# Two edits in a one-core layer kernel: where the experts' down bias is added, and how the first loads and modulation weights are laid out

## The chip, the cores and the metric

The kernel runs on one core of one Trainium2 chip. The metric is the device time of one execution in microseconds (us). All data are 32-bit floats in HBM at the start, and the output goes back to HBM.

## The reference, cut to what matters

The program computes two transformer layers on 256 tokens of width 1024. The first layer normalises x, modulates it with vectors that come from a conditioning row c, mixes tokens (an RWKV recurrence and a block attention), and ends in a mixture of 32 experts with 4 experts for each token. The second layer has another attention and a feed-forward of width 4096. What the change touches is this:

```python
mods = jax.nn.silu(c) @ w_ada + b_ada                  # (1, 6*1024)
shift1, scale1, gate1, shift2, scale2, gate2 = jnp.split(mods[:, None, :], 6, axis=-1)
h = rms_norm(x, norm1_g) * (1.0 + scale1) + shift1
proj = h @ w_in
...
def expert_block(args):                                # rows of one expert
    tok, e = args
    gu = h[tok] @ w_gate_up[e] + b_gate_up[e]
    gate = jnp.minimum(gu[:, :D_FF], SWIGLU_LIMIT)
    up = jnp.clip(gu[:, D_FF:], -SWIGLU_LIMIT, SWIGLU_LIMIT)
    act = (up + 1.0) * gate * jax.nn.sigmoid(SWIGLU_ALPHA * gate)
    return act @ w_down[e] + b_down[e]
...
# each row times its routing weight, summed over a token's four experts
```

## The kernel before, in words

Every engine has its own hand-written program, and the engines meet at semaphores. The order of the work is the order of each program; no planner stands behind it. SyncE (SP) issues nearly all weight loads on its own DMA queue, and ScalarE (ACT) issues the small ones on a second queue. Both queues are served by the same 16 DMA engines.

**The front.** ACT issues x first (L1419), then 21 small loads of parameter rows into `prow` and `prow2` (L1422 to L1438), then the four pieces of the LoRA weights `wl` (L1440), the router weights `w_rout` (L1444, rows of 128 bytes), its bias, and the experts' first biases `bgu` (L1447). Only then does it compute. SP walks through the list `PRO` of 22 pieces (L308, L362): first the four pieces of w_ada that hold shift1 and scale1, then w_in, with the other pieces of w_ada between. They go through four slots of a ring in SBUF, so piece n waits until piece n-4 is used (`pro_freed`, L355, on `halves_used`), and mem_2 is loaded ahead of piece 4 (L368). Each of the first four pieces is a block of 512 columns of all 1024 rows of w_ada: 128 partitions by 8 row segments of 2 KB, some 2 MB.

TensorE (PE) turns x (L572), waits for all parameter rows and turns them (L577), adds up the squares of x (L584), and then multiplies silu(c) by each piece of w_ada as it arrives (L592 to L610). The silu is 32 equal columns, so that four matmuls for four row blocks k run side by side in four column groups of the array; their four partial sums are turned and added by VectorE (DVE) with a reduce for each piece (`ada_sum`, L1797). When the modulation is whole (`mods_ready`), ACT and DVE scale the normalised x (L1467, L1811), and the first projection (`proj`, L627, matmuls at L643) starts when the first piece of w_in is there.

**The expert loop.** After the router, the kernel works through 32 items, one for each expert (64 rows of capacity; every expert needs one pass here). The ring has nine slots of 2 MB and an expert has six pieces, four of w_gate_up and two of w_down. The first nine pieces are loaded ahead (L395 ff.), the others when a slot is freed (`freed`, on `e_gu` and `e_down`). For one item PE runs the bias of gate and up (L1103: a row `one_e` with a single one picks row e of `bgu`), gate and up (L1110), the gather of the item after next (L1047), the scatter of the item before (`scatter`, L1058: it multiplies the 64 rows by their routing weights and adds them into banks 4 to 7 of PSUM), some transposes, and the down projection (L1146). DVE makes the row `one_e` for the next item with `expert_row` (L2087), ahead of its wait for `e_selturn` in the loop (L2156).

**The down bias** is added once, before the loop: the routing weights of all 32 experts are turned (L1075 to L1078), DVE copies them to `gt` (L2127), and eight matmuls with 32 rows (`down_bias`, L1068 and L1084, matmul at L1070) start the sums of banks 4 to 7 with b_down times the routing weights. Just before and after stand the first gather, `turn_x(1)`, and the waits for `npass_ready` and `wtT_ready`:

```python
            gather(1)
            pe.wait_ge(*at("wt_ready"))
            for i in range(TT):
                last = tr(B(1)[0:E_N, i * P:(i + 1) * P], wt[:, i, :])
            last.then_inc(*mark("wt_turned"))
            turn_x(1)
            pe.wait_ge(*at("npass_ready"))
            pe.wait_ge(S("ada_summed"), 7)
            pe.wait_ge(*at("wtT_ready"))
            pe.wait_ge(S("b_down_in"), 16)
            down_bias(range(KT))
```

A matmul in 32-bit floats is two records in the profile. Transposes of all stages have the line of their helper, L568, and loads that of theirs, L353 for SP and L1412 for ACT.

## Time and profile before

| | us |
|---|---|
| median of 3 runs (1594.67 to 1599.12) | 1597.52 |
| the profiled execution, its own time | 1595.94 |
| its span in the profile | 1594.2 |
| PE busy | 1512.1 (95%) |
| DVE busy | 369.2 (23%) |
| ACT busy | 285.0 (18%) |
| DMA | 503.24 MB, mean 316 GB/s |

The page names the busy time of each engine, and PE leads with 95%. Yet its share is an average over stages, and the matmuls' ends are modelled. The kernel has three large stages: up to about 320 us the first layer up to the router, then the expert loop to 1236 us, and then the second layer. Times in the rows below are microseconds from the start of the span; "<-" names what ended an idle time. A row by stretches has start and end, the length, the busy time and number of instructions of PE, its weight loads, DVE, ACT and POOL in this order (or of PE alone), then the granted clock of TensorE as a share of 2.4 GHz, the busy share of the DMA engines, and the GB/s they moved. The record of the granted clock begins at 23.7 us; the rows show 1.00 before that whatever the engine did.

### The profile page before, as it was taken

To read this page: it belongs to the slowest core of one execution; us is meant where nothing else is said; L and a number is where in the kernel's file an instruction comes from. 1 tells how busy PE (TensorE), PEld (TensorE's weight loads), DVE (VectorE), ACT (ScalarE), POOL (GpSimd) and SP (SyncE) were. 2 spreads that over 40 slices of the span, in tenths; PEclk is the share of its full clock that TensorE was granted. 3 is DMA by queue.
4 is the path that set the end of the run, shared out by engine and by line. 5 is a ranking of instruction groups with operands and counts; after the bars stand their busy time and mean duration, and the time that the engine had idled before them with its cause. 6 is when DMAs were issued, how large, how long until landed. Compare 5 with 4: busy or idle time off the path is not lost.

```text
span 1594.2 us, 20391 instructions
## 1 busy us (share of the span) xinstructions
PE 1512.1 (95%) x8382; PEld 780.1 (49%) x8383; DVE 369.2 (23%) x712; ACT 285.0 (18%) x451; POOL 34.6 (2%) x86
## 2 busy tenths in 40 slices
PE   5999899999999999999999989989999999999998
PEld 3876686733333333333333333333333875888443
DVE  2476442322111111111112112112111233301003
ACT  2123411311111111111111111111111231100000
POOL 5000120000000000000000000000000000000000
PEclk9999998999999999999999999999999999999999
DMA  9856203889999999999999999999999641444420
GB/s 347 293 208 224 94 4 116 372 339 429 428 428 429 428 428 428 430 428 429 428 428 428 429 430 428 429 428 428 428 430 411 244 153 59 160 157 159 158 105 27
DMA packets 75038, 503.24 MB, mean 316 GB/s; under 512 B 5278, under 2 KB 8496, under 8 KB 50416
## 3 DMA queue, kind: packets, MB, share of 16 engines
q1 hardware_dynamic: 72240, 498.22, 76.1%
q10 hardware_dynamic: 2752, 4.34, 0.8%
q8 instruction: 37, 0.61, 0.2%
q14 instruction: 9, 0.07, 0.0%
HBM read 501.49 MB, written 1.05 MB: 315 GB/s over the span
## 4 chain that ended last, share of the span: by engine, by line
PE 70%; DMA 25%; DVE 2%; ACT 1%; ACTq 1%; issue 0%; SPq 0%; DVEq 0%
DMA ring<-in_w_gate_up 24%; PE psum L1110 15%; PE psum L1146 10%; PE psum L1375 6%; PE psum L1390 5%; PE psum L643 5%; PE psum L1197 3%; PE psum L1063 3%; PE psum L568 2%; PE psum L1047 2%; PE psum L981 2%; PE psum L1332 2%; PE psum L1400 2%; PE psum L1103 1%; PE psum L690 1%; PE psum L1347 1%
## 5 line engine op out<-in xcount | busy, mean ns | idle before, releaser
L1110 PE MATMUL psum<-ring,work 128*64 128x512 f32 x2048 | 456.5, 597 | 40.3 <-DMA ring<-in_w_gate_up 40.3
L1110 PEld LDWEIGHTS psum<-ring,work 128*64 128x64 f32 x2048 | 140.8, 137 | 354.7 <-issue 272.7
L1146 PE MATMUL psum<-ring,work 128*64 128x512 f32 x1024 | 226.8, 595 | 1.0
L2145 DVE TENSOR_SCALAR work<-psum 128x512 f32<-128x512 f32 x32 | 22.1, 692 | 623.7 <-PE psum L1110 623.7
L1146 PEld LDWEIGHTS psum<-ring,work 128*64 128x64 f32 x1024 | 70.8, 137 | 136.4 <-issue 127.8
L1657 ACT ACTIVATE work<-work 128x512 f32<-128x512 f32 x32 | 20.1, 629 | 440.7 <-DVE work L2145 440.7
L1375 PE MATMUL psum<-xT,ring 128*128 128x256 f32 x448 | 96.9, 379 | 0.0
L1375 PEld LDWEIGHTS psum<-xT,ring 128*128 128x128 f32 x448 | 85.0, 190 | 11.5
L1390 PE MATMUL psum<-ring 128*128 128x512 f32 x192 | 82.6, 592 | 0.0
L643 PE MATMUL psum<-ring 128*128 128x256 f32 (+1 forms) x368 | 81.0, 382 | 1.1 <-DMA ring<-in_w_in 1.1
L643 PEld LDWEIGHTS psum<-ring 128*128 128x128 f32 (+1 forms) x368 | 68.9, 188 | 14.0 <-issue 2.1
L1063 PE MATMUL psum<-work 64*128 64x256 f32 x528 | 65.9, 389 | 0.7 <-ACT work L1663 0.7
L1063 PEld LDWEIGHTS psum<-work 64*128 64x128 f32 x528 | 48.3, 186 | 31.9 <-issue 26.0
L1047 PE MATMUL psum<-tok,work 128*64 128x512 f32 x264 | 62.3, 592 | 0.3 <-DVE work L2083 0.3
L1390 PEld LDWEIGHTS psum<-ring 128*128 128x128 f32 x192 | 36.5, 190 | 45.5 <-issue 45.4
L1663 ACT ACTIVATE work<-psum 128x512 f32<-128x512 f32 x32 | 19.1, 598 | 209.1 <-PE psum L1146 209.1
L1197 PE MATMUL psum<-xT,ring 128*128 128x256 f32 x224 | 49.7, 381 | 0.7 <-DVE xT L2164 0.7
L1643 ACT ACTIVATE yT<-psum 128x512 f32<-128x512 f32 x33 | 35.1, 1064 | 70.1 <-PE psum L1047 70.1
L1197 PEld LDWEIGHTS psum<-xT,ring 128*128 128x128 f32 x224 | 42.1, 190 | 7.6 <-issue 1.8
L1657 ACT ACT_TABLE_LOAD x32 | 41.1, 1283 | 0.9 <-issue 0.3
L1047 PEld LDWEIGHTS psum<-tok,work 128*64 128x64 f32 x264 | 18.9, 137 | 37.5 <-issue 37.5
L1103 PE MATMUL psum<-bgu,work 32*64 32x512 f32 x256 | 35.7, 627 | 0.0
(434 smaller groups left out, 1265.1 us busy)
## 6 DMA issues: line engine op xcount, KB each, us to landing
ring<-in_w_gate_up SPq DMA_DIRECT2D x128, 2048.0 KB, 36.5
ring<-in_w_down SPq DMA_DIRECT2D x72, 2048.0 KB, 39.7
ring<-in_w_ada SPq DMA_DIRECT2D x12, 2048.0 KB, 12.6
ring<-in_w_up SPq DMA_DIRECT2D x8, 2048.0 KB, 7.5
ring<-in_w_in SPq DMA_DIRECT2D x6, 2048.0 KB, 8.3
ring<-in_w_out SPq DMA_DIRECT2D x4, 2048.0 KB, 8.4
ring<-in_w_in_sb SPq DMA_DIRECT2D x4, 2048.0 KB, 22.8
ring<-in_w_mem_kv SPq DMA_DIRECT2D x1, 2048.0 KB, 9.2
```

The source lines that it names most:

```text
L568: return nc.tensor.transpose(o, i, ident[0:n, 0:n])
L643: last = mm(bank2(bank)[0:m, jj, :], w[:, k, j * P:j * P + m], hT[:, k, :], start=k == 0, stop=k == KT - 1)
L1047: last = mm(B(0)[CAP * h:CAP * (h + 1), :], sel[:, ti, :], tok[:, ti, 512 * h:512 * (h + 1)], start=ti == 0, stop=ti == TT - 1)
L1063: last = mm(bank2(4 + m // 2)[:, m % 2, :], ye[CAP * h:CAP * (h + 1), c * P:(c + 1) * P], selT[CAP * h:CAP * (h + 1), :], start=False, sto ...
L1103: mm(B(1 + u)[CAP * h:CAP * (h + 1), :], one_e[r0:r0 + E_N, :], bgu[r0:r0 + E_N, :], start=True, stop=False)
L1110: ins = mm(B(1 + u)[CAP * h:CAP * (h + 1), :], xe[:, k % 4, k // 4, :], w[:, k % 2, c0:c0 + 512], start=False, stop=k == KT - 1)
L1146: last = mm(B(3)[CAP * h:CAP * (h + 1), :], act[:, k % 4, k // 4, :], w[:, k % 4, 512 * h:512 * (h + 1)], start=k == 0, stop=k == KT - 1)
L1197: last = mm(bank2(b)[:, jj, :], post_w(n)[:, k, c0 + jj * P:c0 + (jj + 1) * P], xT[:, k, :], start=k == 0, stop=k == KT - 1)
L1375: last = mm(bank2(b)[:, jj, :], w[:, k, c0:c0 + P], xT[:, k, :], start=k == 0, stop=k == KT - 1)
L1390: last = mm(B(4 + 2 * i + h), hid[:, k, i * P:(i + 1) * P], down_piece(n)[:, kk_, 512 * h:512 * (h + 1)], start=k == 0, stop=False)
L1643: A(by_four(x_tm), B(0).rearrange("p (q c) -> p q c", c=4), ACT.Copy).then_inc(S("e_xtm"), 1)
L1657: A(sgm, gt, ACT.Sigmoid, scale=1.702).then_inc(S("e_sig"), 1)
```

## The change

It has two parts.

In the expert loop the eight matmuls ahead of the loop, the transposes of the routing weights and DVE's copy of them go. Instead each item starts the sums of its down projection with two matmuls, one for each half of the columns: the row `one_e` picks row e of `b_down`. `one_e` is therefore needed until the down projection has begun, and DVE writes the next one at the end of its round, after a wait on `e_down`. Banks 4 to 7 now start with a product of zeros (`zero`, with the cleared `selT` and `ye`): two such matmuls before `turn_x(1)` and two after it, with the wait for `npass_ready` moved ahead of `turn_x(1)`.

In the front x moves from ACT's queue to the head of SP's, and ACT's queue begins with c, b_ada and norm1_g. These 64 rows are turned first, ahead of x, and ACT makes the sigmoid of c ahead of its copies of x. The other parameter rows follow into a tile of their own and are turned after the modulation. The LoRA weights go to SP's queue behind piece 5, and the router weights, its bias and `bgu` behind piece 9. Each of the first four pieces of w_ada is now 256 whole rows cut at 2048 columns, row segments of 8 KB. The four column groups of one bank now hold four different blocks of 512 columns and add up over all k, so one copy, four transposes and one addition on DVE take the place of four rounds of them.

The diff, without the lists of milestone names, the counters that follow from them, and the loads that only change their tile:

```diff
+N_FIRST = ROW["norm2_g"]
...
-        def pe_ada(x):
-            return x if x < 4 else x - 5
+        def ada_rows(s):
+            return ring[:, s, :].rearrange("p (k n) -> p k n", k=2)
...
+            load(tok[:, :, :], a["x"][0].rearrange("(i p) d -> p i d", p=P), S("x_in"))
...
-                if kind == "ada":
+                if kind == "ada" and i < 4:
+                    load(ada_rows(s), a["w_ada"][0, 2 * P * i:2 * P * (i + 1), 0:2048].rearrange("(k p) n -> p k n", p=P),
+                         S(f"pro_in{s}"))
+                elif kind == "ada":
                     load(slot8(s), chunk_cols(a["w_ada"][0], 512 * i, 512), S(f"pro_in{s}"))
...
+                if n == 5:
+                    load(wl[0:LOW, 0, :], a["rwkv_w_up"][0], S("wl_in"))
+                    load(wl[LOW:P, 0, :], a["rwkv_a_up"][0], S("wl_in"))
+                    load(wl[:, 1, :], a["rwkv_g_up"][0, 0:P, :], S("wl_in"))
+                    load(wl[0:GLOW - P, 2, :], a["rwkv_g_up"][0, P:GLOW, :], S("wl_in"))
+                if n == 9:
+                    load(w_rout[:, :, :], a["w_router"][0].rearrange("(k p) n -> p k n", p=P), S("rout_in"))
+                    load(b_rout[:, :], a["b_router"], S("rout_in"))
+                    for q in range(4):
+                        load(bgu[E_N * q:E_N * (q + 1), :], a["b_gate_up"][0, :, 512 * q:512 * (q + 1)], S("bgu_in"))
...
-            g_.memset(prow, 0.0).then_inc(S("pool_stage"), 1)
+            g_.memset(prow3, 0.0).then_inc(S("pool_stage"), 1)
...
+            pe.wait_ge(S("par_first_in"), 16 * 3)
+            tr(B(1)[:, 0:N_FIRST], prow[0:N_FIRST, :], N_FIRST).then_inc(*mark("par_turned"))
             pe.wait_ge(S("x_in"), 16)
             for b in range(4):
                 for k in (2 * b, 2 * b + 1):
                     for i in range(TT):
                         last = tr(bank2(4 + b)[:, k % 2, i * P:(i + 1) * P], tok[:, i, k * P:(k + 1) * P])
                 last.then_inc(S("x_turned"), 1)
-            pe.wait_ge(S("par_in"), 16 * N_PAR_DMA)
-            tr(B(1)[:, 0:N_ROWS], prow[0:N_ROWS, :], N_ROWS)
-            last = tr(B(1)[:, N_ROWS:N_ROWS + N_ROWS2], prow2[0:N_ROWS2, :], N_ROWS2)
-            last.then_inc(*mark("par_turned"))
...
-            for n in range(5):
-                if n < 4:
-                    arrived(n)
-                    if n >= 2:
-                        pe.wait_ge(S("ada_copied"), n - 1)
-                    w = slot8(pro_slot(n))
-                    for k in range(KT):
-                        q = 32 * (k % 4)
-                        last = mm(B([0, 4][n % 2])[q:q + 32, :], silc[:, k, :], w[:, k, :], start=k < 4, stop=k >= 4)
-                        if k % 4 == 3:
-                            last.then_inc(S("halves_used"), 1)
-                if n >= 1:
-                    m = n - 1
-                    pe.wait_ge(S("ada_copied"), m + 1)
-                    if m >= 2:
-                        pe.wait_ge(S("ada_summed"), m - 1)
-                    for j in range(4):
-                        last = tr(B(5 + m % 2)[:, j * P:(j + 1) * P], ada_sb[m % 2][:, j * P:(j + 1) * P])
-                    last.then_inc(S("ada_turned"), 1)
+            for n in range(4):
+                arrived(n)
+                w = ada_rows(pro_slot(n))
+                for kk in range(2):
+                    k = 2 * n + kk
+                    for cg in range(4):
+                        last = mm(B(0)[32 * cg:32 * (cg + 1), :], silc[:, k, :], w[:, kk, 512 * cg:512 * (cg + 1)],
+                                  start=k == 0, stop=k == KT - 1)
+                    last.then_inc(S("halves_used"), 1)
+            pe.wait_ge(S("ada_copied"), 1)
+            for j in range(4):
+                last = tr(B(5)[:, j * P:(j + 1) * P], ada_sb[:, j * P:(j + 1) * P])
+            last.then_inc(*mark("mod_turned"))
+            pe.wait_ge(S("par_in"), 16 * N_PAR_DMA)
+            n3 = N_ROWS - N_FIRST
+            tr(B(1)[:, N_FIRST:N_ROWS], prow3[0:n3, :], n3)
+            tr(B(1)[:, N_ROWS:N_ROWS + N_ROWS2], prow2[0:N_ROWS2, :], N_ROWS2).then_inc(*mark("par2_turned"))
...
-            def down_bias(ms):
-                for m in ms:
-                    mm(bank2(4 + m // 2)[:, m % 2, :], b_down[:, m * P:(m + 1) * P], gt[0:E_N, 0:T],
-                       start=m % 2 == 0, stop=False, skip_group_check=True)
+            def zero(b):
+                mm(B(b), selT[:, 0:P], ye, start=True, stop=False, skip_group_check=True)
 
             pe.wait_ge(S("h2tok_d"), 4)
             gather(1)
-            pe.wait_ge(*at("wt_ready"))
-            for i in range(TT):
-                last = tr(B(1)[0:E_N, i * P:(i + 1) * P], wt[:, i, :])
-            last.then_inc(*mark("wt_turned"))
+            pe.wait_ge(*at("zeroed"))
+            zero(4)
+            pe.wait_ge(*at("npass_ready"))
+            zero(5)
             turn_x(1)
-            pe.wait_ge(*at("npass_ready"))
-            pe.wait_ge(S("ada_summed"), 7)
-            pe.wait_ge(*at("wtT_ready"))
+            pe.wait_ge(S("ada_summed"), 3)
+            zero(6)
+            zero(7)
             pe.wait_ge(S("b_down_in"), 16)
-            down_bias(range(KT))
             pe.wait_ge(S("bgu_in"), 16 * 4)
...
                     pe.wait_ge(S("e_actT"), g + 1)
+                    for h in range(2):
+                        mm(B(3)[CAP * h:CAP * (h + 1), :], one_e[0:E_N, :], b_down[:, 512 * h:512 * (h + 1)],
+                           start=True, stop=False)
                     for k in range(KT):
                         if k % 4 == 0:
                             landed(4 + k // 4)
                         w = ring[:, slots[4 + k // 4], :].rearrange("p (k n) -> p k n", k=4)
                         for h in range(2):
                             last = mm(B(3)[CAP * h:CAP * (h + 1), :], act[:, k % 4, k // 4, :],
-                                      w[:, k % 4, 512 * h:512 * (h + 1)], start=k == 0, stop=k == KT - 1)
+                                      w[:, k % 4, 512 * h:512 * (h + 1)], start=False, stop=k == KT - 1)
...
-            dma(tok[:, :, :], a["x"][0].rearrange("(i p) d -> p i d", p=P), S("x_in"))
+            n_dma = 0
+            for name, key in [("c", "c"), ("b_ada", "b_ada"), ("norm1_g", "norm1_g")]:
+                src = rows(key)
+                dma(prow[ROW[name]:ROW[name] + src.shape[0], :], src, S("par_first_in"))
             ac.wait_ge(S("pool_stage"), 1)
-            n_dma = 0
-            for name, key in [("b_ada", "b_ada"), ("c", "c"), ("norm1_g", "norm1_g"), ("norm2_g", "norm2_g"),
+            for name, key in [("norm2_g", "norm2_g"),
                               ("w0", "rwkv_w0"), ("a0", "rwkv_a0"), ("k_k", "rwkv_k_k"), ("k_a", "rwkv_k_a"),
                               ("r_k", "rwkv_r_k"), ("ln_g", "rwkv_ln_g"), ("ln_b", "rwkv_ln_b")]:
                 src = rows(key)
-                dma(prow[ROW[name]:ROW[name] + src.shape[0], :], src, S("par_in"))
+                dma(prow3[ROW[name] - N_FIRST:ROW[name] - N_FIRST + src.shape[0], :], src, S("par_in"))
...
-            dma(wl[0:LOW, 0, :], a["rwkv_w_up"][0], S("wl_in"))
-            dma(wl[LOW:P, 0, :], a["rwkv_a_up"][0], S("wl_in"))
-            dma(wl[:, 1, :], a["rwkv_g_up"][0, 0:P, :], S("wl_in"))
-            dma(wl[0:GLOW - P, 2, :], a["rwkv_g_up"][0, P:GLOW, :], S("wl_in"))
-            dma(w_rout[:, :, :], a["w_router"][0].rearrange("(k p) n -> p k n", p=P), S("rout_in"))
-            dma(b_rout[:, :], a["b_router"], S("rout_in"))
-            for q in range(4):
-                dma(bgu[E_N * q:E_N * (q + 1), :], a["b_gate_up"][0, :, 512 * q:512 * (q + 1)], S("bgu_in"))
-
+            ac.wait_ge(*at("par_turned"))
+            ch.link(A(par[:, 0:N_FIRST], B(1)[:, 0:N_FIRST], ACT.Copy))
+            A(sigc[:, :], par[:, ROW["c"]:ROW["c"] + KT], ACT.Sigmoid).then_inc(*mark("sigc_ready"))
             for n, b in enumerate((4, 6)):
                 ac.wait_ge(S("x_turned"), b - 3)
                 A(xT[:, 2 * (b - 4):2 * (b - 4) + 2, :], bank2(b), ACT.Copy).then_inc(S("xcopy_a"), 1)
                 A(hT[:, 2 * (b - 4):2 * (b - 4) + 2, :], bank2(b), ACT.Square).then_inc(S("xsq_a"), 1)
-            ac.wait_ge(*at("par_turned"))
-            ch.link(A(par[:, :], B(1)[:, 0:N_ROWS + N_ROWS2], ACT.Copy))
-            A(sigc[:, :], par[:, ROW["c"]:ROW["c"] + KT], ACT.Sigmoid).then_inc(*mark("sigc_ready"))
             ac.wait_ge(*at("xss"))
             ac.wait_ge(*at("eps_ready"))
             A(rstd[:, :], B(3)[:, 0:T], ACT.Sqrt, bias=small[:, 0:1], scale=1.0 / D).then_inc(S("rs_ready"), 1)
-            for n in range(4):
-                ac.wait_ge(S("halves_used"), 2 * n + 2)
-                if n >= 2:
-                    ac.wait_ge(S("ada_turned"), n - 1)
-                A(ada_sb[n % 2], B([0, 4][n % 2]), ACT.Copy).then_inc(S("ada_copied"), 1)
+            ac.wait_ge(S("halves_used"), 8)
+            A(ada_sb, B(0), ACT.Copy).then_inc(S("ada_copied"), 1)
+            ac.wait_ge(*at("par2_turned"))
+            A(par[:, N_FIRST:N_ROWS + N_ROWS2], B(1)[:, N_FIRST:N_ROWS + N_ROWS2], ACT.Copy)
...
-            for n in range(4):
-                ada_sum(n, 5 + n % 2)
-            ve.wait_ge(S("ada_summed"), 4)
-            ch.link(V.tensor_tensor(mods[:, 0:16], mods[:, 0:16], par[:, 0:16], ALU.add))
+            ve.wait_ge(*at("mod_turned"))
+            ch.link(V.tensor_tensor(mods[:, 0:16].rearrange("p (g j) -> p j g", g=4),
+                                    B(5).rearrange("p (j g r) -> p j g r", j=4, g=4)[:, :, :, 0],
+                                    par[:, 0:16].rearrange("p (g j) -> p j g", g=4), ALU.add))
...
-            ve.wait_ge(*at("wt_turned"))
-            V.tensor_copy(gt[0:E_N, 0:T], B(1)[0:E_N, 0:T]).then_inc(*mark("wtT_ready"))
...
-                expert_row(e)
                 ve.wait_ge(S("e_selturn"), g + 1)
                 V.tensor_copy(selT, B(1)[:, 0:T]).then_inc(S("e_selT"), 1)
                 select_weighted(e, p)
+                ve.wait_ge(S("e_down"), g * 2 + 1)
+                expert_row(e)
```

## Rows read from the trace of the kernel before

**Rows 1.** The chain that ended last, in the front (start us, length us, what):
```profile
18.84 5.89 PE psum L584 x16
...
27.06 12.05 DMA ring<-in_w_in
...
39.25 38.54 PE psum L643 x176
```

**Rows 2.** The same chain in the expert loop:
```profile
352.81 13.88 PE psum L1110 x64
...
379.71 13.88 PE psum L1110 x64
...
652.61 38.21 DMA ring<-in_w_gate_up
...
711.31 38.24 DMA ring<-in_w_gate_up
...
1228.01 7.11 PE psum L1146 x32
```

**Rows 3.** Stretches of all engines, two in the front and one in the loop:
```profile
26.00:50.00 24.00, 21.22 (x137) 12.52 (x130) 8.27 (x16) 5.07 (x10) 1.32 (x3) 1.00 1.05 388
340.00:360.00 20.00, 19.97 (x108) 7.73 (x106) 3.70 (x9) 4.15 (x5) 0.00 (x0) 1.00 1.00 428
2.00:32.80 30.80, 16.83 (x90) 10.31 (x90) 7.62 (x9) 8.58 (x13) 20.24 (x68) 1.00 1.06 360
```

**Rows 4.** The timeline of the front (start us, busy us, engine, line, operation):
```profile
8.95 0.32 ACTq L1412 DMA_DIRECT2D ring<-in_ln_ffn_b  x1
...
15.43 1.28 ACT L1451 ACT_TABLE_LOAD   x1 [15.43 <-issue]
...
20.29 0.21 ACT L1455 ACTIVATE sigc<-par 128x8 f32<-128x8 f32 x1
...
26.65 0.37 SPq L353 DMA_DIRECT2D ring<-in_mem  x1
...
32.82 1.92 PE L600 MATMUL psum<-ring,silc_t 128*32 128x512 f32 x16 [1.49 <-DMA ring<-in_w_ada]
...
36.84 2.08 ACT L1467 ACTIVATE ring<-ring,mods,sc 128x256 f32<-128x256 f32 x4 [1.43 <-DVE sc L1806]
```

**Rows 5.** The timeline just ahead of the expert loop:
```profile
313.70 1.94 PE L1047 MATMUL psum<-tok,work 128*64 128x512 f32 x8 [0.26 <-DVE work L2083]
...
315.67 1.04 ACT L1643 ACTIVATE yT<-psum 128x512 f32<-128x512 f32 x1 [3.59 <-PE psum L1047]
...
315.77 0.16 DVE L2118 TENSOR_SCALAR last_pass<-cnt 1x32 int32<-1x32 f32 x1
...
316.76 0.66 PE L568 MATMUL psum<-ident,yT 128*128 128x128 f32 x4 [0.80 <-ACT yT L1643]
...
317.91 4.91 PE L1070 MATMUL psum<-work 32*128 32x256 f32 x16 [0.50 <-DVE work L2128]
...
322.75 1.98 PE L1103 MATMUL psum<-bgu,work 32*64 32x512 f32 x8
...
324.66 5.68 PE L1110 MATMUL psum<-ring,work 128*64 128x512 f32 x20
```

**Rows 6.** The page's group of full-array matmuls with 512 columns:
```profile
L1390 PE MATMUL psum<-ring 128*128 128x512 f32 x192 | 82.6, 592 | 0.0
```

**Rows 7.** Stretches again, of the engines PE alone:
```profile
256.00:266.00 10.00, 9.13 (x30) 0.52 0.01 2
318.00:320.00 2.00, 2.00 (x10) 1.00 1.05 451
320.00:328.00 8.00, 8.00 (x26) 0.57 0.36 153
328.00:330.00 2.00, 2.00 (x12) 1.00 0.00 0
```

**Rows 8.** The timeline in the loop, the last item's gate and up bias:
```profile
1205.65 1.09 PE L1103 MATMUL psum<-bgu,work 32*64 32x512 f32 x8
```

More of the change, by code:

```diff
@@ L63 @@
 N_ROWS2 = 32
+N_FIRST = ROW["norm2_g"]
 MILESTONES = {
     "tensor": [
-        "par_turned", "xss", "lora_w", "lora_a", "lora_g", "kkss", "bonss", "qkss", "vturned",
-        "biki_turned", "shift_0", "shift_1", "wsh_spread", "logits", "ranks", "wt_turned",
+        "par_turned", "xss", "mod_turned", "par2_turned", "lora_w", "lora_a", "lora_g", "kkss", "bonss", "qkss", "vturned",
+        "biki_turned", "shift_0", "shift_1", "wsh_spread", "logits", "ranks",
     ],
@@ L245, in build @@
         prow2 = view(ws, 128, [P])
+        prow3 = view(ws, 256, [P])
         wl = view(work_f, 2056, [3, RW])
@@ L252, in build @@
         silc = silc_t[:, :, :]
-        ada_sb = [view(ws, 8192 + 512 * i, [512]) for i in range(2)]
+        ada_sb = view(ws, 8192, [512])
         ada_late = view(tok_f, 0, [512])
@@ L777, in ada_turn @@
             def ada_turn(x, bank):
-                pe.wait_ge(S("ada_copied"), pe_ada(x) + 1)
+                pe.wait_ge(S("ada_copied"), x - 7)
                 for j in range(4):
@@ L1021, in _ @@
             pe.wait_ge(*at("shift_out"))
-            pe.wait_ge(S("ada_summed"), 5)
+            pe.wait_ge(S("ada_summed"), 1)
             second_norm(0)
```

17 lines of the change are left out of this document (9 added, 8 removed).

## The prediction

> **What bounds the kernel now.** I read the chain that ended last first, then the timeline where the chain changes its owner, then the stretches for rate and clock. The page's 95% for PE is a mean over stages, so it can't say what a shorter front or a longer item is worth.
>
> In the front the chain goes from the sum of squares (18.84) over the load of w_in (27.06, landed at 39.1) to the projections, where PE runs 38.5 us without a stop [rows 1]. The fourth piece of w_ada arrives at 32.82, and its product ended a wait for DMA [rows 4]. From 26 to 50 us the DMA engines are full at 388 GB/s [rows 3]. So the front is bound by bytes. What starts the first projection earlier moves everything behind it, since PE is the chain from there to the router.
>
> In the expert loop one item takes PE 26.90 us (379.71 less 352.81) [rows 2]. An expert is 12.58 MB, at 428 GB/s [rows 3] 29.4 us, and two experts take 58.70 us (711.31 less 652.61) [rows 2]. PE is faster than the loads. It lives off the nine pieces loaded ahead until 649 us, then waits for a piece of w_gate_up in each item. The loads run without a gap once the first slot is freed, and the loop's end hangs on that moment. At 328 to 330 us nothing is moved, and the 153 GB/s over the 8 us before are 1.2 MB, done near 323 [rows 7]: the nine slots are full and the queue waits for PE. Each microsecond by which the first slot is freed earlier is a microsecond off the end, until the 7 us of that gap are used up.
>
> **The front, step by step.** By their shapes x and four pieces are 9.44 MB, the parameter rows 0.07 MB, and the loads that leave ACT's queue (LoRA, router, biases) 0.98 MB, together 10.49 MB. From 2 to 32.8 us the mean is 360 GB/s [rows 3], so they are done at 2 + 29.1 = 31.1, and the fourth piece counts as arrived 1.7 us later. After the change 0.98 MB stand behind piece 5 or later. If the rest runs at the 388 GB/s of the 2 KB rows, it takes 24.5 us and the fourth piece is there at 28.2, 4.6 us earlier. But segments are 8 KB now. The loop's 16 KB segments run at 428. With a fixed cost for each segment, per engine 2 KB take 84.5 ns and 16 KB 612 ns, so 8 KB take 311 ns, an estimate of 420 GB/s. Then 1.12 MB at 388 and 8.39 MB at 420 take 22.9 us, and the piece is there at 26.6, **6.2 us earlier**. I take this, as the two ends bracket it by rates that the trace shows.
>
> The Trainium skill (DMA: Bandwidth & Descriptors, Why small descriptors are slow) speaks against so much: it gives a fixed cost of some 3 cycles for each packet, with 32 bytes a beat. From 2 KB to 8 KB that is 3%, and the step would be 5.3 us by it. The rows differ by 10% between 2 and 16 KB, where this rule gives 4%.
>
> Is anything else late instead? ACT's small loads end at 9.27 [rows 4]; without x (some 0.5 us) at 8.8. Then come table, copy, second table and sigmoid, 3.2 us, and the four copies and squares of x, 2.1 us (the same work takes 15.43 to 20.50 now [rows 4]). The squares are summed from 14.1 on instead of 18.84 [rows 1]. With 5.9 us for them and 1.9 for each piece [rows 1, 4], piece 0 is used at 22, pieces 0 to 2 at 26. mem_2 and w_in are released by piece 0, now at 26.65 [rows 4], then at 22; the queue holds pieces until 25, so no gap opens. The way from the fourth piece to the scaled x is 6.1 us (32.82 to 38.92 [rows 4]) and to w_in's landing 6.3 us; both stay, a few tenths less for the dropped reductions. The par copy on ACT and the later transposes lie beside DVE's work. The LoRA weights (needed near 77) and router weights (near 269) have tens of microseconds to spare; their ten issues delay later pieces on SP by some 3 us where the queue isn't full.
>
> **Ahead of the loop.** PE's gather ends at 315.64, x is copied at 316.71, the counts are ready at 315.93 [rows 5]. A zero matmul is 2 records of 0.43 us (82.6 us for 192 [rows 6]), 0.86 us. Two of them fill 315.6 to 317.4, `turn_x` (0.66 us, now from 316.76 [rows 5]) ends near 318.0, two more at 319.7. So the first item's bias matmul starts at 319.7 instead of 322.75 [rows 5]: 3.1 us for 4.91 us of down bias removed. What was waited for, DVE's copy of the weights, is gone. The moved wait on the counts is covered by zero(4); without that cover it would cost 0.3 us.
>
> The clock comes on top. From 320 to 328 the granted clock is 0.57 on average, 1.2 GHz for 6.9 of 8 us, with PE busy throughout; in 318 to 320 it is 2.4 [rows 7]. Before this fall PE ran short waits, transposes and the 32-row down bias. The other long fall, 256 to 266 [rows 7], also follows thin matmuls. The change puts full-array products there. Now the first slot is freed after 16 records of L1110: 20 take 5.68 from 324.66 [rows 5], less 4 of 0.217 (13.88 for 64 [rows 2]) gives 329.5. Without a fall it would be 319.7 + 1.09 [rows 8] + 3.47 = 324.3, **5.2 us earlier**. With a fall at the same place it is 319.7 + 1.0 + 16 x 0.43 = 327.6, only 1.9 earlier. I take no fall, for what precedes it.
>
> The Trainium skill (TensorE: Matmul & The Clock Gate, Part 1) lets the clock fall after idleness and keeps it up while the engine is busy. The trace agrees only in part, since PE was busy ahead of this fall too. By that rule the fall goes as well, for the idle time is filled.
>
> **Each item.** Two matmuls more, side by side in two halves of columns as in L1110: 4 records of 0.217 are 0.87 us. The ends are 0.55 (half of L1103's 1.09 [rows 8]) and 1.73 (one after the other [rows 6]). PE's item grows to 27.8 us, below 29.35: the extra time falls into the wait for pieces, except after the last piece of w_gate_up of the last expert. So **0.9 us** once, 0.5 to 1.7. The loads stay gapless, PE merely runs dry later, near item 19 instead of 12. `expert_row` now waits for the first half of the down projection, with `select` of the next round queued behind it on DVE. The row is needed one half projection (3.5 us) later, the select some 20 us later.
>
> **Sum.** -6.2 - 5.2 + 0.9 = -10.5 us. Against the profiled execution (1595.94, span 1594.2) that is 1585.4. That execution lies 1.6 below the median 1597.52, so I state 1587.0 for the median.
>
> **The rivals.**
> - The clock falls again at the start of the loop. For it: such falls come at several places, and the transposes and small ranks stay. Against it: the thin matmuls go. -6.2 - 1.9 + 0.9 = -7.2, hence 1590.3. Chance 0.3.
> - TensorE stays at 1.2 GHz through the front. Its first matmuls are slow now, and the sum of squares moves to 14.1. Were it slow up to the last piece, squares would take 6.9 us and each piece 3.8: piece 3 is used at 36, against 34.74 now, and the front gains nothing. -5.2 + 0.9 = -4.3, hence 1593.2. Against it: PE is busier there than before. Chance 0.1.
> - Slower: PE becomes the bound of the loop. Its place is the start of the down projection and the next item's wait for `one_e`. From the first bias matmul (322.75) to the end (1235.1 [rows 2]) are 912.3 us for 32 items, 28.5 each. Above 1.6 us extra per item PE sets the end; with the earlier start (3.1 + 6.2 + some clock) the kernel is slower from 2.0 us on. The matmuls (0.9) and a stalled row (say 1.6) give 29.4, 32 times 0.9 above 28.5 is +29, less 11: 1615. Against it: DVE is idle there. Chance 0.05.
> - The edits don't do what they say: the 8 KB segments are no faster. -8.9, hence 1588.6; it lies inside the first case.
>
> **How the numbers follow.** The first case has 0.55. About 0.3% (4.8 us) is what a measurement of this kernel can tell from no change, so the line is at 1592.7. The first two cases are faster, the third is "same" or close to it, the fourth slower: 0.85, 0.1, 0.05. The range goes down to 1581 (front 7 us, 0.55 per item, and the long fall of 256 to 266, which costs 4.8 us, partly gone) and up to 1593 (the third case, or the second with no faster segments and 1.7 per item).
>
> **What would show it.** In the new profile: the squares' matmuls at 14, the fourth piece's product near 26.6, L643 from 33; no idle stretch of DMA before 45 us. At the loop: L1103 some 9.3 us earlier than 322.75, clock 1.00 in the 8 us behind it, the first DMA traffic 11 us earlier. Periods of 27.8 until near 850 us, then 29.35. The forecast is wrong if PE has no DMA wait in late items, or if a gap in the DMA opens at 20 to 30 us.

## The result, and the profile after

| | before | after |
|---|---|---|
| median (lowest to highest) | 1598.32 us (1594.67 to 1599.23), 4 executions | 1585.56 us (1583.09 to 1586.21), 4 executions |
| profiled execution | 1595.94 us, span 1594.2 | 1583.09 us, span 1581.3 |
| PE busy | 1512.1 (95%) | 1528.8 (97%) |

The ratio on record is 0.9934, with an interval of [0.9919, 0.9948], so the change takes off 10.5 us, 8 to 13 by the interval. The two medians of the table differ by 12.8. The forecast was 1587.0 (1581 to 1593) and -10.5. Later comparisons on other occasions had the kernel before at 1594.4, 1593.6 and 1595.1 us, so below mainly the ratios, taken against executions of the same occasion, are compared. The changed kernel once more, in the last of them, had 0.9939 [0.992, 0.9957], 9.7 us.

Some line numbers moved: L655 is the projection (L643 before), L598 the squares (L584), L612 the product with w_ada (L600), L1112 the item's gate and up bias (L1103), L1119 its gate and up (L1110), L1059 the gather (L1047), L784 the late products with w_ada (L772), L1158 the down projection (L1146), L1151 the new pair of down bias, L1081 the products of zeros, L584 the transposes (L568).

The chain that ended last, changed kernel (start us, length us, what), answers to [rows 1, 2]:

```profile
14.35 5.34 PE psum L598 x16
...
22.02 10.93 DMA ring<-in_w_in
33.09 38.54 PE psum L655 x176
...
339.65 13.88 PE psum L1119 x64
...
367.56 13.88 PE psum L1119 x64
...
817.93 35.22 DMA ring<-in_w_gate_up
...
874.65 37.24 DMA ring<-in_w_gate_up
933.37 37.23 DMA ring<-in_w_gate_up
...
1215.20 7.04 PE psum L1158 x32
```

The first projection starts 6.16 us earlier (39.25 less 33.09). One item takes PE 27.91 us (367.56 less 339.65), 1.01 more than before. The chain passes to the loads with the one that landed at 853.15 (817.93 and 35.22). Before, the first such load landed at 690.82 (652.61 and 38.21). From then on two experts take 58.72 us (933.37 less 874.65), as before. The last down projection starts 12.81 us earlier (1228.01 less 1215.20).

The timeline of the front, changed kernel (start us, busy us, engine, line, operation), answers to [rows 4]:

```profile
0.80 0.46 SPq L355 DMA_DIRECT2D tok<-in_x  x1
1.30 2.28 SPq L355 DMA_DIRECT2D ring<-in_w_ada  x4
...
8.21 0.34 PE L584 MATMUL psum<-ident,ring 64*128 64x64 f32 x1 [8.21 <-DMA ring<-in_norm_g]
...
21.61 0.37 SPq L355 DMA_DIRECT2D ring<-in_mem  x1
...
26.91 1.92 PE L612 MATMUL psum<-ring,silc_t 128*32 128x512 f32 x16 [1.93 <-DMA ring<-in_w_ada]
```

The fourth piece ends PE's wait at 26.91 (32.82 before). PE still waits for it (1.93 us), so the front is still bound by bytes. Stretches of all engines, changed kernel (start and end, length, the busy time of five engines, granted clock, DMA share, GB/s), answer to [rows 3]:

```profile
4.00:26.00 22.00, 14.57 (x81) 9.08 (x81) 7.06 (x7) 6.70 (x10) 17.48 (x55) 1.00 1.02 420
26.00:50.00 24.00, 21.75 (x115) 16.05 (x116) 9.63 (x20) 3.77 (x8) 2.89 (x8) 1.00 1.05 372
```

In the first of these stretches, with rows of 8 KB, the engines move 420 GB/s. Where pieces with 2 KB rows follow, the rate is 372.

The timeline ahead of the loop, changed kernel, answers to [rows 5, 8]:

```profile
297.09 5.34 PE L784 MATMUL psum<-ring,silc_t 128*32 128x512 f32 x32
...
304.71 1.94 PE L1059 MATMUL psum<-tok,work 128*64 128x512 f32 x8 [0.26 <-DVE work L2088]
306.58 1.98 PE L1081 MATMUL psum<-work 128*128 128x512 f32 x4
...
308.40 0.60 PE L584 MATMUL psum<-ident,yT 128*128 128x128 f32 x4
308.84 1.88 PE L1081 MATMUL psum<-work 128*128 128x512 f32 x4
310.65 1.09 PE L1112 MATMUL psum<-bgu,work 32*64 32x512 f32 x8
311.67 6.66 PE L1119 MATMUL psum<-ring,work 128*64 128x512 f32 x30
```

PE doesn't wait any more between the gather and the first item. The gather (304.71 and 1.94) ends at 306.65 and the item's bias matmul starts 4.0 us later (7.1 before, 315.64 to 322.75), now in 1.09 us instead of 1.98. Stretches of PE there, changed kernel, answer to [rows 7]:

```profile
312.00:320.00 8.00, 8.00 (x40) 1.00 0.70 266
314.00:316.00 2.00, 2.00 (x12) 1.00 0.08 33
316.00:318.00 2.00, 2.00 (x12) 1.00 0.83 221
```

The granted clock is 1.00 from the first item on (0.57 from 320 to 328 before). The nine slots are full near 314, the loads start again near 317. Before, nothing was moved from 328 to 330, and they started again near 331:

```profile
330.00:332.00 2.00, 2.00 (x12) 1.00 0.72 180
```

### The profile page after: what moved, and what is told of

It is laid out like the page before. It is cut to its first block, busy times and chain, and to the rows that moved or that the text cites. A ratio compares the mean times of both kernels' runs of the same rounds, so it can differ in the third digit from the quotient of the medians.

```text
span 1581.3 us, 20591 instructions
## 1 busy us (share of the span) xinstructions
PE 1528.8 (97%) x8489; PEld 782.7 (49%) x8490; DVE 374.3 (24%) x707; ACT 283.1 (18%) x449; POOL 36.7 (2%) x86
## 4 chain that ended last, share of the span: by engine, by line
PE 79%; DMA 17%; DVE 2%; ACT 1%; issue 0%; ACTq 0%; SPq 0%; DVEq 0%
PE psum L1119 19%; DMA ring<-in_w_gate_up 16%; PE psum L1158 11%; PE psum L1387 6%; PE psum L1402 5%; PE psum L655 5%; PE psum L1075 3%; PE psum L1209 3%; PE psum L584 3%; PE psum L1059 3%; PE psum L993 2%; PE psum L1344 2%; PE psum L1412 2%; PE psum L1151 2%; PE psum L1112 2%; PE psum L702 1%
## 5 line engine op out<-in xcount | busy, mean ns | idle before, releaser
L1119 PE MATMUL psum<-ring,work 128*64 128x512 f32 x2048 | 449.4, 594 | 15.5 <-DMA ring<-in_w_gate_up 15.5
L1119 PEld LDWEIGHTS psum<-ring,work 128*64 128x64 f32 x2048 | 142.1, 137 | 320.5 <-issue 285.2
L1158 PE MATMUL psum<-ring,work 128*64 128x512 f32 x1024 | 226.8, 595 | 0.0
L1158 PEld LDWEIGHTS psum<-ring,work 128*64 128x64 f32 x1024 | 70.8, 137 | 153.8 <-issue 153.8
L655 PE MATMUL psum<-ring 128*128 128x256 f32 (+1 forms) x368 | 80.4, 380 | 0.6 <-DMA ring<-in_w_in 0.6
L655 PEld LDWEIGHTS psum<-ring 128*128 128x128 f32 (+1 forms) x368 | 68.3, 186 | 12.7 <-issue 1.3
L1059 PE MATMUL psum<-tok,work 128*64 128x512 f32 x264 | 62.3, 592 | 0.3 <-DVE work L2088 0.3
L2093 DVE TENSOR_SCALAR work<-ones,id 128x64 f32<-128x64 f32 x33 | 8.4, 255 | 137.7 <-PE psum L1158 137.6
L1059 PEld LDWEIGHTS psum<-tok,work 128*64 128x64 f32 x264 | 19.0, 137 | 37.5 <-issue 37.5
```

Source lines behind the costliest of these rows:

```text
L655: last = mm(bank2(bank)[0:m, jj, :], w[:, k, j * P:j * P + m], hT[:, k, :], start=k == 0, stop=k == KT - 1)
L1059: last = mm(B(0)[CAP * h:CAP * (h + 1), :], sel[:, ti, :], tok[:, ti, 512 * h:512 * (h + 1)], start=ti == 0, stop=ti == TT - 1)
L1119: ins = mm(B(1 + u)[CAP * h:CAP * (h + 1), :], xe[:, k % 4, k // 4, :], w[:, k % 2, c0:c0 + 512], start=False, stop=k == KT - 1)
L1158: last = mm(B(3)[CAP * h:CAP * (h + 1), :], act[:, k % 4, k // 4, :], w[:, k % 4, 512 * h:512 * (h + 1)], start=False, stop=k == KT - 1)
```

## The experiments

**1 and 2: each part alone, with both kernels again beside them.** The first has the down bias per item and the zero products, and the front of before. The second has the new front, and `down_bias` ahead of the loop. The first's core, against the kernel before, is this; the second has the rest of the change and none of it:

```diff
+            zero(4)
+            pe.wait_ge(*at("npass_ready"))
+            zero(5)
             turn_x(1)
...
+            zero(6)
+            zero(7)
...
-            down_bias(range(KT))
...
+                    for h in range(2):
+                        mm(B(3)[CAP * h:CAP * (h + 1), :], one_e[0:E_N, :], b_down[:, 512 * h:512 * (h + 1)],
+                           start=True, stop=False)
```

> The kernel before with only the down bias moved into the items (zero products ahead of the loop, expert_row at the end of DVE's round); the front is untouched. Theory (my sum): the first item's gate and up bias starts 3.1 us earlier than before, the granted clock no longer falls there (2.1 us more), each item is 1.0 us longer on PE (27.9 instead of 26.9) and this shows once at the end: 4.2 us faster than before in all, DMA waits of the loop beginning near item 18 instead of 12. Rival (the clock falls again at the start of the loop): 1 to 2 us faster only. Rival (the longer item counts in every item): more than 20 us slower.

> The changed kernel with the down bias back ahead of the loop as before; only the front is changed. Theory: the first projection starts at 33.1 instead of 39.25 and this shift of 6.2 us arrives whole at the end, 6 us faster. If the fall of the granted clock at 99 to 106 us, which the changed kernel's profile does not show, is gone because of the front (another place in time of the thin matmuls), it is 8.5 to 9 us; if its absence was chance, 6. Rival (the front's gain is swallowed by the nine preloaded slots of the loop): under 3 us.

> The kernel before, unchanged, profiled once more. If the falls of the granted clock depend on the work alone, they stand at the same places as in the first profile: 98.8 to 105.7, 256 to 266, 307 to 310 and 320.7 to 327.5 us. If they depend on chance too, at least one is missing, new or moved by some 3 us, and the time differs by 1 to 3 us with it.

> The changed kernel, unchanged, profiled once more. If the work alone sets the clock: no fall between 92 and 98 us and none in the 8 us behind the start of the loop, first item at 310.7 us. If chance has a part, the fall near 95 us is back (first item 2.5 to 3 us later) or one stands behind the start of the loop.

Measured: the bias alone 1592.22 us, ratio 0.9989 [0.9979, 0.9998]; the front alone 1589.47, 0.9963 [0.9949, 0.9977]; before again 1592.83 and after again 1585.79, one execution each. The front alone is worth 5.9 us (0.37%), as the 6.2 of the forecast has it. The bias alone is worth 1.8 us (0.3 to 3.3), less than the 4.3 net of the sum and the 4.2 expected, which lie outside the interval. The two ratios together give 7.7, the whole change 10.5 and 9.7. With intervals of 1.5 and 2.2 us on either side of the parts, the gap between them and the whole is not beyond the measurement, and it stays open whether anything but chance is in it. The profile of the bias alone shows more than its median: its way from the first projection to the ranks ahead of the loop (272.0 us, 39.44 to 311.48) is as long as in the first profile of the kernel before (272.1, 39.25 to 311.35), and its span is 3.5 us shorter (1590.7 and 1594.2).

The two repeats were to show whether the falls of the granted clock depend on the work alone. They don't. The kernel before, run again, hasn't the fall at 98 to 106 us, and has the one at the start of the loop. The changed kernel, run again, has a fall at 94 to 98 (0.59), and one in the front from 26 to 30, where its fourth product takes 3.45 us and its first projection starts at 34.26. It has none at the start of the loop.

The traces tell more than the times. The timeline of the front alone, just ahead of the loop, and under it its stretches of PE:

```profile
310.17 5.65 PE L1082 MATMUL psum<-work 32*128 32x256 f32 x16 [0.48 <-DVE work L2133]
315.76 1.98 PE L1115 MATMUL psum<-bgu,work 32*64 32x512 f32 x8
```

```profile
312.00:320.00 8.00, 8.00 (x27) 0.59 0.39 163
```

With the 32-row down bias the clock falls at the start of the loop, also in the kernel before when it ran again. That makes three profiles, and run 6 adds a fourth with products over 32 rows. In the ten profiles with the zero products over 128 rows (the changed kernel three times, the bias alone, and runs 3, 4, 5, 7, 9 and 10) the clock stays at 1.00 for 8 us from the first item on. This is the stretch of the bias alone, where the first item starts at 319.77:

```profile
312.00:320.00 8.00, 7.73 (x39) 1.00 1.01 432
```

**3: 2 KB rows in the new front.** Each of the four pieces is loaded by four DMAs, one for each block of 512 columns. The waits count the additional DMAs. Layout in SBUF, product and everything else stay.

```diff
-                    load(ada_rows(s), a["w_ada"][0, 2 * P * i:2 * P * (i + 1), 0:2048].rearrange("(k p) n -> p k n", p=P),
-                         S(f"pro_in{s}"))
+                    for cg in range(4):
+                        load(ada_rows(s)[:, :, 512 * cg:512 * (cg + 1)],
+                             a["w_ada"][0, 2 * P * i:2 * P * (i + 1), 512 * cg:512 * (cg + 1)].rearrange(
+                                 "(k p) n -> p k n", p=P), S(f"pro_in{s}"))
```

> The changed kernel, but each of the first four pieces of w_ada is loaded by four DMAs of 512 columns (segments of 2 KB as before) instead of one with segments of 8 KB; bytes, places and order are the same. Theory (a fixed cost for each segment, 388 against some 420 GB/s): the fourth piece's product starts at 28.4 instead of 26.9 us, the first projection at 34.6 instead of 33.1, and 1.5 us arrive at the end. Rival (the rate is the same for both): no change. By the rule of a page of the Trainium skill weighed in the prediction it would be about 0.9 us.

Measured: 1589.78 us, 0.9968 [0.9957, 0.998]. The timeline of its front, and under it a stretch of all engines to compare with the 420 GB/s of the changed kernel:

```profile
1.31 15.32 SPq L355 DMA_DIRECT2D ring<-in_w_ada  x16
...
28.55 3.00 PE L614 MATMUL psum<-ring,silc_t 128*32 128x512 f32 x16 [3.23 <-DMA ring<-in_w_ada]
32.24 4.62 PE L586 MATMUL psum<-ident,ring 128*128 128x128 f32 x22 [0.70 <-ACT ring L1468]
36.70 3.62 PE L657 MATMUL psum<-ring 128*128 128x256 f32 x16
```

```profile
4.00:26.00 22.00, 15.55 (x81) 9.70 (x81) 7.15 (x7) 6.70 (x10) 17.55 (x53) 1.00 1.05 387
```

The fourth piece comes at 28.55 instead of 26.91. For its arrival the length of the rows is therefore worth 1.6 us, which is the difference between the 4.6 and the 6.2 of the forecast. The four pieces are four times as many DMAs here, so length and number of DMAs are changed together. The first projection is 3.6 us later (36.70), more than the piece, because in this execution the fourth product (3.00 for 1.92) and the transposes ran at 1.2 GHz. The longer wait for the piece stands ahead of them, but the changed kernel's repeat had the same fall with 8 KB rows.

In the times the step is larger than expected: the ratio is 0.0029 to 0.0034 above the changed kernel's two, 4.6 to 5.4 us, where 1.5 were expected. The profile has 6.7 us (spans of 1588.0 and 1581.3). Of these 3.6 are the later projection and 2.1 the way from there to the ranks, less than the repeats of one kernel differ by. How much of the fall in the front belongs to the 2 KB rows was not measured.

The Trainium skill (DMA: Bandwidth & Descriptors, Why small descriptors are slow) gives a fixed cost of some 3 cycles for each packet, from which 8 KB would gain an estimated 3%. The runs gained 8% (387 to 420 GB/s), and the measurement decides.

**4: the small loads back on ACT's queue.** LoRA weights, router weights with their bias, and `bgu` are issued by ACT behind the parameter rows.

```diff
-                if n == 5:
-                    load(wl[0:LOW, 0, :], a["rwkv_w_up"][0], S("wl_in"))
...
-                if n == 9:
-                    load(w_rout[:, :, :], a["w_router"][0].rearrange("(k p) n -> p k n", p=P), S("rout_in"))
...
+            dma(wl[0:LOW, 0, :], a["rwkv_w_up"][0], S("wl_in"))
...
+            dma(w_rout[:, :, :], a["w_router"][0].rearrange("(k p) n -> p k n", p=P), S("rout_in"))
+            dma(b_rout[:, :], a["b_router"], S("rout_in"))
...
```

> The changed kernel, but the LoRA and router weights, the router's bias and bgu are issued by ACT behind the parameter rows again, as in the kernel before (0.98 MB ahead of the fourth piece of w_ada, and ACT's computing begins 6 us later). Theory (the front is bound by bytes): the fourth piece arrives 3 to 4 us later and the first projection starts near 37.5, 4 to 5 us slower than the changed kernel. Rival (the segments or the order of x made the gain): under 1 us.

Measured: 1599.67 us, 1.004 [1.0025, 1.0055], slower than the kernel before. The few microseconds expected were far off. ACT's timeline in this kernel (ACTq is the issue of a DMA):

```profile
10.86 0.44 ACTq L1414 DMA_DIRECT2D w_rout<-in_w_router  x1
11.33 13.06 ACTq L1414 DMA_DIRECT2D b_rout<-in_b_router  x1
24.42 2.51 ACTq L1414 DMA_DIRECT2D bgu<-in_b_gate_up  x4
26.96 1.28 ACT L1454 ACT_TABLE_LOAD   x1 [26.96 <-issue]
```

and PE's:

```profile
32.00 5.98 PE L588 MATMUL psum<-ring,ones 128*128 128x256 f32 x16 [19.95 <-ACT ring L1459]
...
49.25 3.04 PE L645 MATMUL psum<-ring 128*128 128x256 f32 x13 [0.63 <-DMA ring<-in_w_in]
```

A single issue held ACT's program for 13.06 us, so the copies and squares of x behind it came late, PE stood idle for 19.95 us, and the first projection started at 49.25, 16.2 us later than in the changed kernel. The ratios differ by as much (0.0101 to 0.0106, 16 to 17 us). So the step "the loads that leave ACT's queue" is worth far more than its 0.98 MB in this new front. Behind x and four pieces that SP had issued by 3.5 us, ACT didn't issue them without a stall. In the kernel before, where SP's four issues took from 0.80 to 15.44, the same issue took 1.40 us.

**5: which load stalls ACT.** As 4, with only the router weights (1024 rows of 128 bytes) left behind piece 9 on SP.

```diff
-            dma(w_rout[:, :, :], a["w_router"][0].rearrange("(k p) n -> p k n", p=P), S("rout_in"))
+                if n == 9:
+                    load(w_rout[:, :, :], a["w_router"][0].rearrange("(k p) n -> p k n", p=P), S("rout_in"))
```

> The changed kernel with the LoRA weights, the router bias and the experts' first biases issued by ACT behind the parameter rows, but the router weights (1024 rows of 128 bytes) left in SP's queue behind piece 9. Theory (the 1024 small rows are what filled ACT's queue, so that the issues behind them waited 13 us): no stall of ACT, its table load at 15 to 18 us, the first projection 3 to 5 us later than in the changed kernel (0.85 MB in front of the fourth piece), 1588 to 1591. Rival (any load of that size behind SP's filled queue stalls ACT): an issue of several us again, and 1593 to 1600.

Measured: 1593.15 us, 0.9988 [0.9977, 0.9999]; the profiled execution 1588.57. ACT's timeline:

```profile
10.91 0.30 ACTq L1416 DMA_DIRECT2D b_rout<-in_b_router  x1
11.23 1.73 ACTq L1416 DMA_DIRECT2D bgu<-in_b_gate_up  x4
13.00 1.28 ACT L1455 ACT_TABLE_LOAD   x1 [13.00 <-issue]
```

The same issue takes 0.30 us, so the load of the router weights was what the next issue had waited for. Whether by the shortness of its rows or by their number was not separated. The first projection starts at 38.10, 5.0 us later than in the changed kernel, and the fourth piece's product at 31.98, 5.1 later, behind a wait for its load. So the delay is the load's, and ACT's 4.5 us of later start don't set it. The bytes account for less than half: 0.85 MB at 420 GB/s are 2.0 us. The rest is the rate, 373 GB/s in this kernel with the same 8 KB rows:

```profile
4.00:26.00 22.00, 11.90 (x49) 8.95 (x53) 3.99 (x6) 6.70 (x10) 17.39 (x59) 1.00 1.02 373
```

The small loads ahead of the fourth piece thus cost more than their bytes. Which of them lower the rate was not tried. The kernel is some 6.5 us slower than the changed kernel beside it (1586.65), 1.5 more than that start, and above the 1588 to 1591 expected.

**6: zero products with 32 rows.** One edit: the contraction of `zero` goes over 32 rows instead of 128. Number and length of the matmuls are the same, and so is PE's busy time at the full clock.

```diff
-                mm(B(b), selT[:, 0:P], ye, start=True, stop=False, skip_group_check=True)
+                mm(B(b), selT[0:E_N, 0:P], ye[0:E_N, :], start=True, stop=False, skip_group_check=True)
```

> The changed kernel with the four zero products on 32 rows of the array instead of 128 (same columns, same length, still zeros). Theory (what keeps the clock at 2.4 GHz at the start of the loop is how much of the array works): the granted clock falls to 1.2 GHz again within the 8 us behind the first item's start, as in all three profiles with the old down bias, and 1.5 to 2.5 us are lost. Rival (what counts is that PE has no idle stretch there): no fall, no change.

Measured: 1587.83 us, 0.996 [0.9948, 0.9972]. Its timeline and its stretch:

```profile
309.35 1.98 PE L1081 MATMUL psum<-work 32*128 32x512 f32 x4
311.26 0.65 PE L584 MATMUL psum<-ident,yT 128*128 128x128 f32 x4
311.85 2.40 PE L1081 MATMUL psum<-work 32*128 32x512 f32 x4
314.18 1.98 PE L1112 MATMUL psum<-bgu,work 32*64 32x512 f32 x8
```

```profile
312.00:320.00 8.00, 8.00 (x22) 0.58 0.60 254
```

PE has no wait in these rows, as in the changed kernel, and yet the clock falls (0.58). The way from the ranks (L1045) to the item's first product of gate and up, 9.3 us in the changed kernel, is 11.1 (304.99 to 316.10), and the item after it is slow too. So what took the fall away is that the products fill the array, not that they fill the time. The ratio is 0.0021 to 0.0026 above the changed kernel's two, 3.3 to 4.1 us, though the intervals overlap. The trace has 3.6: 1.8 on this way, and 1.8 more from the start of the first product of gate and up to that of the last down projection (905.3 against 903.5).

**7: two pairs of down bias in each item.** The bias is added twice, so the output has twice the down bias.

```diff
-                    for h in range(2):
+                    for h2 in range(4):
+                        h = h2 % 2
                         mm(B(3)[CAP * h:CAP * (h + 1), :], one_e[0:E_N, :], b_down[:, 512 * h:512 * (h + 1)],
-                           start=True, stop=False)
+                           start=h2 < 2, stop=False)
```

> The changed kernel with the pair of down bias matmuls issued twice in each item (b_down is added twice, so the output has the down bias doubled). PE's item grows from 27.9 to 28.9 us, still less than the 29.35 us that the loads of one expert take. Theory of the prediction (nine pieces are loaded ahead, so PE sets the end above 28.5 us per item): 32 x 28.9 from the first item's start, about 13 us slower than the changed kernel, and no DMA wait in the loop. Rival (the loads' 29.35 us are the bound, what is below is free): 1.0 us slower, DMA waits remain in the last items.

Measured: 1596.81 us, one execution. The chain in the loop:

```profile
345.08 13.88 PE psum L1119 x64
...
373.85 13.88 PE psum L1119 x64
```

The item takes 28.77 us (373.85 less 345.08), 0.86 more than with one pair, and PE waits for no piece in the whole loop. With a row of its last item,

```profile
1228.84 7.09 PE L1159 MATMUL psum<-ring,work 128*64 128x512 f32 x32
```

the last down projection starts 13.7 us later than in the changed kernel (1215.13 in the same view), of which 9.1 are the loop's (from the first item's start at 315.22 to the end 920.7 us, close to 32 times 28.77, against 911.6). The rest is the way up to the loop in that execution. So the second pair costs 9 us where the first cost about one. This fits the rival on the slow side in place and threshold: at 27.9 us an item's extra time shows once, and at 28.77 the loop takes what 32 items take. Values between were not tried.

**8 to 10: full products ahead of the other long fall.** The changed kernel has a fall from 247 to 257 us, behind thin matmuls with three short waits. Products of `ident` with the router weights into bank 0, which nothing reads, were put at the three waits, two or four at each. The first kernel's:

```diff
+            def fill():
+                for _ in range(2):
+                    mm(B(0)[:, 0:T], ident[:, :], w_rout[:, :, :].rearrange("p k n -> p (k n)"), start=True, stop=True,
+                       skip_group_check=True)
...
+            fill()
             group_centre(1, 0)
```

> The changed kernel once more, as the measure for the three runs beside it. The earlier executions gave 1585.6 and 1585.8; both theories expect 1584 to 1587, with the long fall of the granted clock near 247 to 257 us again, and none at the start of the loop.

> The changed kernel plus six full-array products of ident with the router weights, whose result nothing reads, two at each of the three waits (0.68, 0.79 and 0.69 us) that PE has in the thin matmuls ahead of 247 us. Six are some 2.6 us, 2.2 of them in idle time. Theory (a stretch that fills little of the array brings the fall): the fall of 247 to 257 goes or comes later and shorter, that stretch is up to 4.6 us shorter, the kernel 1582 to 1584. Rival (the fall comes at its time whatever stands there, or these fills are too few): the fall stays, the kernel is 0 to 1 us slower than the changed kernel.

> The same with four products at each wait, twelve in all, some 5.2 us, 3 more than the idle time holds. Theory: the fall goes, the kernel is 3 us dearer for the fills and 4.6 cheaper for the clock, 1583 to 1585. Rival: the fall stays and the kernel is at 1588 to 1590.

Measured: the changed kernel 1586.65 us (1582.51 to 1588.05), two fills 1586.11, 0.9936 [0.9919, 0.9953], four fills 1586.0, 0.9941 [0.9927, 0.9955]. Stretches of PE, first the changed kernel beside them, then with two fills:

```profile
252.00:258.00 6.00, 5.31 (x14) 0.50 0.00 0
...
240.00:270.00 30.00, 27.12 (x205) 0.83 0.26 84
```

```profile
252.00:258.00 6.00, 6.00 (x46) 1.00 0.01 3
...
240.00:270.00 30.00, 29.28 (x241) 1.00 0.37 129
```

With two fills the long fall is gone. With four a shorter one is left at 240 to 246 (0.72; 240 to 270 has 0.94). From the centring of the first half to the product with w_ada behind it the way is 15.4 us with two fills and 18.1 without (the starts of L921 and L784: 240.94 and 256.35, 240.18 and 258.23). With four it is 19.6 (237.71 and 257.30), longer than without. The medians moved by 0.5 and 0.7 us, less than the measurement can tell, where two to five were expected. The profile of one execution doesn't say why. Other falls move from one execution to the next: with two fills 120 to 150 has a granted clock of 0.89, in the changed kernel's first profile 1.00. The expected gain was not shown.

## Why the prediction was right

- **The front, -6.2 forecast, -6.16 in the profile.** Each step stands: squares at 14.1 forecast, 14.35 seen; fourth piece at 26.6, seen 26.91; piece 0 used by 22, SP goes on at 21.61; projection at 33, seen 33.09. The front alone gives 5.9 us in the times, and run 3 shows the 1.6 us by which the fourth piece comes earlier with the longer rows. The forecast also took 388 GB/s for the 2 KB rows once the small loads are gone, where the front had run at 360, and gave no reason. This is 1.9 of the 6.2 us. Run 3 bears it out with 387, and run 5 shows the rate at 373 with most of the small loads back. The -6.2 holds for the first profile; in the changed kernel's repeat, with the low clock in the front, the first projection comes 5.0 earlier.
- **Ahead of the loop, -5.2 forecast, -5.4 in the profile.** From the start of the last product with w_ada ahead of the ranks to the item's bias matmul are 13.56 us now (297.09 to 310.65) and were 16.67 (306.08 to 322.75). This is the 3.1 of the forecast. The rest is the clock: the 16 records that free the first slot end at 311.67 + 3.47 = 315.1 instead of 329.5. Run 6, with the four profiles over 32 rows against the ten over 128, shows that the reason given (thin products ahead of the fall) was the right one. The rival "the clock falls again", with 0.3, is what run 6 makes of the kernel: 0.996 of the 1597.5 us that the forecast started from is 1591.1, where the rival had 1590.3.
- **Each item, +0.9 forecast.** The new pair takes 1.07 us by its row, the period grows by 1.01. From the freed slot (-14.4) to the last down projection (-12.8) 1.6 us are given back. The last piece of w_gate_up lands 13.9 us earlier (1205.51 for 1219.39), so 1.0 of them is the pair behind it, and some 0.5 is lost among the loads ahead of it, for which no row was found. PE's waits for pieces of w_gate_up fall from 40.3 to 15.5 us, and the first load on the chain lands at 853 (forecast near 850). This is the extra work being taken from idle time:

```profile
PE psum L1119 <- DMA ring<-in_w_gate_up: 15.5, 13, 1.2
```

- **A term the forecast didn't have.** The profiled executions differ by 12.85 us, where the ratio has 10.5. The way from the first projection to the last w_ada product (33.09 to 297.09 and 39.25 to 306.08) is 2.8 us shorter in the profile after, though the change touches little there beside the small loads behind pieces 5 and 9. It takes 264.0, 265.4 and 268.5 us in the three profiles of the changed kernel, and 266.8 and 263.7 in the two of the kernel before, so one kernel differs from itself by more than that. This is chance and no part of the effect: 12.85 less 2.8 is 10.0. It also makes the difference between the 12.1 us by which the first item starts earlier (322.75 and 310.65) and the 9.3 of the forecast. That the ratio agrees with the forecast to the tenth is luck too. Its interval is 8 to 13 us, the repeat had 9.7, and the parts add up to 7.7.
- **The rivals.** TensorE at 1.2 GHz through the front was not seen as a whole, but run 3 shows a piece of it, 30 to 36 us, and the changed kernel's repeat another, 26 to 30. The slow side was far from reached, and run 7 fits its threshold. That the 8 KB rows are no faster fell in run 3. This rival's price was off: it had -8.9 us, and the kernel with 2 KB rows gains 5.1 (3 to 7). The 0.9 us that run 3's expectation has by the page's rule should be 0.7, 5.3 less 4.6.
- **Mis-sized:** what the bias alone is worth. The sum gives 4.3 net, the run 1.8 with an interval up to 3.3, and its profile 3.5.

## What to carry to other kernels

In a loop bound by its loads, compare the engine's period with the loads' before moving work into it: here 1.0 us more an item cost 1 us in all, and a further 0.86 cost 9. Work that merely starts an accumulation is better done by products that fill the array, since a 32-row product of the same length brought the clock down where a 128-row one did not. A load with many tiny rows belongs behind the large ones that are waited for first, on a queue whose engine has nothing else to do. The clock's falls move between executions of one kernel, so a single profile sizes a step of 2 or 3 us badly.

## What had not been expected of the hardware

- **A stalled issue.** The issue behind 1024 rows of 128 bytes took 13.06 us on ACT's queue when SP had issued x and four pieces by 3.5 us, and 0.30 us without these rows (runs 4, 5).
- **The clock falls without any idle time.** In run 6 PE is busy in all of the rows ahead of the fall, with products over 32 rows. The Trainium skill (TensorE: Matmul & The Clock Gate, Part 1) tells of a fall after idleness. Run 4 agrees with that, where PE has nothing to do and the granted clock is at 1.2 GHz:

```profile
16.00:22.00 6.00, 0.00 (x0) 0.00 (x0) 0.00 (x0) 0.00 (x0) 5.05 (x14) 0.51 1.02 367
```

  But idleness isn't the whole. Neither run 6 nor the changed kernel has idle time in the rows ahead of the first item. The clock falls with products over 32 rows and stays at 1.00 with 128.
- **Small loads ahead didn't arrive first.** c, b_ada and norm1_g are issued at 0.80 to 2.6 us and x at 0.80, but the first transposes wait for these rows until 8.21. x, a load of 1 MB, lands 5.2 us after its issue, near 6.0. In the kernel before it took 7.4, until near 8.2. Its transposes start at 8.47, no earlier than before (8.33), as they now stand behind those of the small rows. So x ahead on SP's queue arrived 2.2 us earlier, and the order of the transposes used that up. In run 3, with 2 KB rows beside them, the small rows are there at 6.80. PE still waited for the fourth piece, so the front gained by what stands ahead of that piece, and by its rate.
